# Attention of a streaming encoder step: token tiles taken in pairs of small and large, in groups of four heads

## The reference

```
q, k, v, z, qi, ki, wi = project(rmsnorm(h) @ w_in)       # 8 q heads, 2 kv heads, 8 indexer heads, head size 128
score = sum over indexer heads of wi * relu(qi . ki)      # one score for each query and key
sel   = top_k(score of keys in the query's 64-frame chunk or before, 256 keys; sample: 136)
o     = softmax(q . k[sel] * 128**-0.5) @ v[sel]          # each group of 4 q heads shares a kv head
h     = h + (o * silu(z)) @ w_out
```

## Time and profile before

| | before |
|---|---|
| time, median of 3 runs | 1431.69 us (1431.41 to 1433.59) |
| the profiled execution | 1432.42 us, its span 1430.6 us |
| PE busy | 1370.9 us (96%) |
| DVE busy | 907.0 us (63%) |
| ACT busy | 639.8 us (45%) |
| POOL busy | 671.7 us (47%) |
| attention, first q·k product to last product with v | 448.95 to 636.24 us |

### The profile page before, as it was taken

The page is one execution under the profiler, slowest core; times in us unless marked ns, Lnnn a source line. Parts: engine busy times, 40 slices in busy tenths (PEclk is TensorE's granted clock), DMA queues, the critical chain, the costliest instruction groups (busy, mean ns, idle before and its releaser), DMA issues.

```text
span 1430.6 us, 21114 instructions
## 1 busy us (share of the span) xinstructions
PE 1370.9 (96%) x7996; PEld 1193.2 (83%) x7996; DVE 907.0 (63%) x1638; ACT 639.8 (45%) x1125; POOL 671.7 (47%) x469
## 2 busy tenths in 40 slices
PE   5999999999998999989989999999999999999997
PEld 5999845999986555548879999999999999999786
DVE  4211287999994877533557676777676767677433
ACT  5333365678774655541114534343434343434111
POOL 2466700555554767740023656465656565654100
PEclk9999999999999999999999999999999999999999
DMA  7221100223222400002221101010101010106321
GB/s 226 87 58 45 44 1 1 60 76 93 69 64 75 147 15 20 0 30 84 87 84 48 45 21 60 22 60 22 60 22 60 22 60 21 60 7 208 108 88 67
DMA packets 101587, 86.79 MB, mean 61 GB/s; under 512 B 6480, under 2 KB 90320, under 8 KB 101488
## 3 DMA queue, kind: packets, MB, share of 16 engines
q1 hardware_dynamic: 99856, 80.63, 18.6%
q0 software_dynamic: 1632, 4.82, 0.9%
HBM read 65.46 MB, written 19.97 MB: 60 GB/s over the span
## 4 chain that ended last, share of the span: by engine, by line
PE 45%; DVE 7%; issue 1%; POOL 1%; DMA 1%; ACT 0%; SPq 0%; POOLq 0%; DVEq 0%; ACTq 0%
PE bank L186 27%; PE wide L1565 7%; PE bank L1460 7%; PE wide L1572 1%; DVE levels L1852 1%; DVE states L1888 1%; PE wide L1575 1%; DVE o_rec L1932 1%; DMA rw_raw<-in_rec_w_in 1%; PE wide L1548 1%; POOL o_sums L1764 1%; DVE log_decay L1820 0%; PE wide L1552 0%; DVE k_rec L1861 0%; DVE last_state L1888 0%
## 5 line engine op out<-in xcount | busy, mean ns | idle before, releaser
L186 PE MATMUL bank<-hn_hi,rw_hi 128*128 128x352 f32 x768 | 251.2, 327 | 6.7 <-DVE h_rows L1241 4.7
L186 PE MATMUL bank<-hn_hi,rw_lo 128*128 128x352 f32 x768 | 247.3, 322 | 0.0
L186 PE MATMUL bank<-hn_lo,rw_hi 128*128 128x352 f32 x768 | 247.0, 322 | 0.0
L186 PE MATMUL bank<-hn_hi,w_hi 128*128 128x352 f32 x648 | 210.3, 324 | 3.3 <-ACT relu L681 2.5
L186 PE MATMUL bank<-hn_lo,w_hi 128*128 128x352 f32 x648 | 207.8, 321 | 0.0
L186 PE MATMUL bank<-hn_hi,w_lo 128*128 128x352 f32 x648 | 207.7, 320 | 0.0
L950 POOL TENSOR_SCALAR probs<-probs,low 128x128 f32<-128x128 f32 (+8 forms) x72 | 127.6, 1775 | 63.3 <-DVE low L1085 63.1
L186 PEld LDWEIGHTS bank<-hn_hi,rw_hi 128*128 128x128 f32 x768 | 144.6, 188 | 8.8 <-DVE h_rows L1241 4.9
L186 PEld LDWEIGHTS bank<-hn_lo,rw_hi 128*128 128x128 f32 x768 | 145.1, 189 | 0.0
L186 PEld LDWEIGHTS bank<-hn_hi,rw_lo 128*128 128x128 f32 x768 | 144.6, 188 | 0.0
L730 POOL TENSOR_TENSOR swapped<-swapped,sin 128x352 f32<-128x352 f32 x57 | 55.4, 971 | 186.6 <-ACT swapped L677 125.8
(11 more groups left out here) (239 smaller groups left out, 2944.1 us busy)
## 6 DMA issues: line engine op xcount, KB each, us to landing
rw_raw<-in_rec_w_in SPq DMA_DIRECT2D x32, 512.0 KB, 4.0
w_raw<-in_att_w_in SPq DMA_DIRECT2D x27, 512.0 KB, 3.9
q_rotated<-relu SPq DMA_DIRECT2D x24, 176.0 KB, 1.9
xin<-in_x_prompt SPq DMA_DIRECT2D x8, 512.0 KB, 3.7
wo_raw<-in_att_w_out SPq DMA_DIRECT2D x4, 1024.0 KB, 8.5
x_again<-in_x_prompt SPq DMA_DIRECT2D x8, 512.0 KB, 4.2
residual<-h_rows SPq DMA_DIRECT2D x8, 512.0 KB, 2.9
wf_raw<-in_rec_w_out SPq DMA_DIRECT2D x4, 1024.0 KB, 10.2
```

The source lines that it names most:

```text
L186: last = pe.matmul(out, l, r, start=n == 0, stop=n == len(passes) - 1)
```

## The change

The list of items is built from groups of four heads: for each pair of tiles (0 and 7, 1 and 6, 2 and 5, 3 and 4) heads 0 to 3 of the small tile, heads 0 to 3 of the large one, heads 4 to 7 of the small one, heads 4 to 7 of the large one; the sample's two groups come last. Each group gets its queries by its own DMA of 256 KB. Groups 0 and 1 (heads 0 to 3 of tiles 0 and 7) are loaded when query head 6 is stored, groups 2 and 3 when all are, 4 to 7 after the first item, and from 8 on each when its buffer has been read; there are now eight query buffers of four heads, each with a semaphore. The buffers of groups 0 and 1 lie in new space behind the other tensors of the block. DVE marks tile 7 ahead of its first item, as soon as the rows of k are stored (L1073), and then, one step an item, tiles 6, 5, 2, 4, 3 and the sample. The work of an item is unchanged, and so are LAG, RING, the number of banks and the positions (48, 56; 52, 60) at which the output projection's weights are cast and split.

```diff
--- before.py
+++ after.py
@@ -132,7 +132,7 @@
         S["w_raw"] = space("w_raw", [P, W_SLOTS, KT, P])
         S["w_lo"] = Space(nc, w_at)("w_lo", [P, W_SLOTS, KT, P], F32R)
         S["w_hi"] = space("w_hi", [P, W_SLOTS, KT, P], F32R)
-        S["q_first"] = Space(nc, space.at)("q_first", [P, 2, HEADS, P])
+        S["q_first"] = [None, None] + [Space(nc, space.at + j * GROUP * P * 4)(f"q_first{2 + j}", [P, GROUP, P]) for j in range(2)]
         S["cos"] = space("cos", [P, T])
         S["sin"] = space("sin", [P, T])
 
@@ -267,6 +267,7 @@
     S["wi"] = space("wi", [P, NT, IH])
     S["kiTs"] = space("kiT_sample", [P, KEYS_S])
     S["signs"] = space("signs", [P, D], BF16)
+    S["q_first"][0:2] = [space(f"q_first{j}", [P, GROUP, P]) for j in range(2)]
     S["swapped"], S["relu"] = swapped, relu
     stages = [input_norm(nc, S), attention_project(nc, S), attention(nc, S)]
     with nc.Block() as block:
@@ -499,6 +500,7 @@
         after.setdefault(min(last_of_tile[c - SLOTS] + 2, last_of_tile[c - 1]), []).append(c)
 
 
+    EARLY = HEADS - 2
     BITS, PACE = 31, 5000
     rope_last = max(i for i, u in enumerate(units) if u[0] == "rope")
     counted_after, time = {}, 0
@@ -577,8 +579,16 @@
                     if i in rows_before:
                         store_rows(rows_before[i])
                 done = last_of_tile[c - SLOTS] + 1
+                if tiles[c - SLOTS] == EARLY * P:
+                    first = 3 * (EARLY + 1)
+                    sp.wait_ge(q_stored[0], 16 * ((first + 1) // 2))
+                    sp.wait_ge(q_stored[1], 16 * (first // 2))
+                    for group in range(2):
+                        load_queries(sp, S, group)
             for stored_q in q_stored:
                 sp.wait_ge(stored_q, 16 * n_q[N] // 2)
+            for group in range(2, 4):
+                load_queries(sp, S, group)
 
         def rows_stored(engine):
             engine.wait_ge(stored[0], 32 * ((NT + 1) // 2))
@@ -879,12 +889,27 @@
     return dict(sync=sync, tensor=tensor, scalar=scalar, gpsimd=gpsimd, vector=vector)
 
 
+def query_groups():
+
+    pairs = [(t, half) for small in range(NT // 2) for half in range(2) for t in (small, SAMPLE - 1 - small)]
+    return pairs + [(SAMPLE, 0), (SAMPLE, 1)]
+
+
+def load_queries(sp, S, group):
+
+    t, half = query_groups()[group]
+    sp.dma_start(S["queries"](group)[:, :, 0:rows(t)],
+                 S["q_dram"][GROUP * half:GROUP * (half + 1), :, span(t)].rearrange("h p t -> p h t")).then_inc(
+                     S["q_in"][group if group < 4 else 4 + group % 4], 16)
+
+
 def attention(nc, S):
 
     sem, ps, wide, pT, q_dram = S["sem"], S["ps"], S["wide"], S["pT"], S["q_dram"]
     gT, kT, v, ident = S["gT"], S["kT"], S["v"], S["ident"]
     kTs, cv, score, opened = S["kTs"], S["cv"], S["score"], S["open"]
-    items = [(t, h) for t in range(NT) for h in range(HEADS)]
+    groups = query_groups()
+    items = [(t, GROUP * half + h) for t, half in groups for h in range(GROUP)]
     N, LAG, RING = len(items), 4, 5
     masks, off = {0: opened[:, 0:P], 1: opened[:, P:3 * P]}, 0
     for t in range(2, NT):
@@ -907,37 +932,32 @@
     mixed, gated, order, inv_done = sem("mixed"), sem("gated"), sem("mark_order"), sem("inv_done")
     counts, limits, sel, bits, marks, ranks = (S[n] for n in ("counts", "limits", "sel", "bits", "marks", "ranks"))
     logits = wide[:].rearrange("p (s b) c -> p s (b c)", s=2)
-    q_in, wo_in = [sem("q_in0"), sem("q_in1")], sem("wo_in")
+    q_in, wo_in = [sem(f"q_in{j}") for j in range(8)], sem("wo_in")
+    S["q_in"] = q_in
     w_out = S["io"]["att_w_out"][0].rearrange("(k p) c -> p k c", p=P)
     space = Space(nc, S["lo_at"])
     probs = space("probs", [P, RING, SEQ])
     low = space("low", [P, 3, N])
-    q_next = space("q_tile", [P, 2, HEADS, P])
-    q_in_first = [sem("q_in_first0"), sem("q_in_first1")]
-
-    def queries(t):
-        return (S["q_first"] if t < 2 else q_next)[:, t % 2]
-
-    def wait_queries(engine, t):
-        if t < 2:
-            engine.wait_ge(q_in_first[t], 16)
-        else:
-            engine.wait_ge(q_in[t % 2], 16 * (t // 2))
+    q_next = space("q_tile", [P, 4, GROUP, P])
+    marked = [SAMPLE - 2] + [t for pair in range(2, NT // 2) for t in (SAMPLE - 1 - pair, pair)] + [SAMPLE]
+
+    def queries(group):
+        return S["q_first"][group] if group < 4 else q_next[:, group % 4]
+
+    S["queries"] = queries
     if True:
         def sync(sp):
-            for t in range(NT):
-                if t == 2:
+            for group in range(4, len(groups)):
+                if group == 4:
                     sp.wait_ge(logits_ready, 1)
-                elif t >= 4:
-                    sp.wait_ge(logits_ready, HEADS * (t - 1))
-                sp.dma_start(queries(t)[:, :, 0:rows(t)],
-                             q_dram[:, :, span(t)].rearrange("h p t -> p h t")).then_inc(
-                                 q_in_first[t] if t < 2 else q_in[t % 2], 16)
-                if t == 3:
-
-                    sp.wait_ge(logits_ready, 2 * HEADS)
+                if group == 8:
+
+                    sp.wait_ge(logits_ready, 4 * GROUP)
                     for ks, cols in weight_pieces():
                         sp.dma_start(S["wo_raw"][:, ks, cols], w_out[:, ks, cols]).then_inc(wo_in, 16)
+                if group >= 8:
+                    sp.wait_ge(logits_ready, GROUP * (group - 3))
+                load_queries(sp, S, group)
             S["rows_stored"](sp)
             sp.wait_ge(S["v_stored"], 32)
             sp.wait_ge(wo_in, 64)
@@ -962,12 +982,16 @@
                     pe.wait_ge(keys_done, 1)
                 if i >= 2:
                     pe.wait_ge(logits_read, i - 1)
-                if h == 0:
-                    wait_queries(pe, t)
+                group = i // GROUP
+                if i % GROUP == 0:
+                    if group < 4:
+                        pe.wait_ge(q_in[group], 16)
+                    else:
+                        pe.wait_ge(q_in[4 + group % 4], 16 * (group // 4))
                 src = kTs if t == SAMPLE else kT
                 for a in range(0, n, 512):
                     e = min(n, a + 512)
-                    last = pe.matmul(logits[0:rows(t), i % 2, a:e], queries(t)[:, h, 0:rows(t)],
+                    last = pe.matmul(logits[0:rows(t), i % 2, a:e], queries(group)[:, i % GROUP, 0:rows(t)],
                                      src[:, h // GROUP, a:e], start=True, stop=True)
                 last.then_inc(logits_ready, 1)
 
@@ -1069,15 +1093,15 @@
                                   gT[:, h:h + 4, span(t)], ALU.mult).then_inc(gated, 1)
 
             dve.wait_ge(S["open_done"], 3)
+            S["rows_stored"](dve)
+            for step in marking(SAMPLE - 1):
+                step()
             dve.wait_ge(*S["units_read"])
-            S["rows_stored"](dve)
+            steps = [step for t in marked for step in marking(t)]
             for i in range(N + 12):
                 if i < N:
-                    t, h = items[i]
-                    if h == 0 and 2 <= t + 1 < NT:
-                        steps = marking(t + 1)
                     shift(i)
-                    if 2 <= t + 1 < NT:
+                    if steps:
                         steps.pop(0)()
                 if 2 <= i <= N + 1:
                     t, h = items[i - 2]
```

## The result

The changed kernel takes 1444.51 us (median of 4 runs, 1443.01 to 1445.66), the kernel before 1432.21 (4 runs, 1431.41 to 1433.59). The ratio is 1.0077, 95% interval 1.0061 to 1.0092: slower by 12.3 us, where 6.7 were forecast. 1444.5 lies in the range (1431 to 1446), but above the forecast's own 1435 to 1441. The profiled execution took 1445.66 us around a span of 1443.9; the one before 1432.42 around 1430.6.

The account below looks back on a forecast made before the run. TensorE, busy 96% of the span, was taken as the bound. Attention: 444.67 + 169.3 work + 29.0 lost = 643.0, 6.7 us later, so 1432.42 + 6.7 - 0.7 = 1438.4 us; forecast 1435 to 1441, range 1431 to 1446.

Parts of the forecast that it names:

- opening: Steps 0 to 7 of attention, bound by VectorE: 4.4 us lost, with step 8 starting at 457.2.
- first switch: Steps 8 to 11, tile 7 to 0: transposes wait for GpSimd's large divisions; 13.6 us long, 8.4 lost.
- 7 to 1, 6 to 1, 6 to 2, 5 to 2: Later changes from large to small tiles: 11.6, 10.2, 10.3, 9.1 us long; 3.7, 2.0, 1.3 and none lost.
- all switches: All changes from a large to a small group in attention: together 15.4 us lost.
- casts: ScalarE's two casts of the output projection's weights, at steps 48 and 56: 1.8 us lost, bounds 0 and 3.8.
- tail from the last q·k: End of attention, behind the last q·k, with three sample divisions in line: 2.6 us lost.
- other steps: The other 40 prompt steps of attention at 0.12 us each: 4.8 us lost.
- the marks' waits: Waits for marks, named with the clock as what could come on top to reach the range's 1446.
- Free; without the cover, 8: VectorE's marking of tile 7 ahead of attention, from 435.9 to 444: no cost, or 8 us without the cover.
- I take it at nothing: TensorE's clock may fall in the opening, hidden beside VectorE's steps: cost nothing, bounds 0 and 2 us.
- slower still, by the clock: Rival: clock falls in the first switch; half clock costs 3.4 us, again behind tile 1; 1442 to 1445; chance 0.25.
- Faster: the pairs even out: Rival: GpSimd works ahead in attention, 16.5 us lost, 1425.9; decided at head 6's division by step 10; chance 0.12.

Follow-up runs that it names:

- a3: The changed kernel with GpSimd dividing only the first 128 columns of each head, the others left undivided: ratio 1.0003 to the kernel before.
- the control: The kernel before with GpSimd dividing only the first 128 columns of each head: ratio 0.9987 to the unedited kernel before.
- a2: The changed kernel with LAG 5 and RING 6, one step more between a head's q·k and its transposes: ratio 1.0031 to the kernel before.
- b1: The changed kernel without tile 7's marking ahead of attention, its scores going in as they are: ratio 1.0056 to the kernel before.
- c1: The changed kernel with its first four q·k products repeated 5, 8, 4 and 4 times to keep TensorE busy: ratio 1.0082 to the kernel before.
- a1: The changed kernel without the pairs and tile 7's early marking: old tile order, early queries per group; 1428.76 us, ratio 0.9949 to the kernel before.
- b4: The changed kernel with its first four groups' query loads all behind the last store, as before: ratio 1.0112 to the kernel before.

## Why the prediction was right in kind and short by 5.6 us

By its own steps, from the start of the first q·k; "lost" is length less PE's work as the prediction had it. The table follows the two profiled executions, which lie 13.2 us apart; the medians lie 12.3 apart.

| step | forecast | measured |
| --- | --- | --- |
| first q·k | 444.67, no DMA wait | 445.00, none |
| opening, lost | 4.4, step 8 at 457.2 | 8.75 (16.85 less 8.1), step 8 at 461.85 |
| first switch, lost | 8.4 (13.6 long) | 8.9 (14.13 long) |
| 7 to 1, 6 to 1, 6 to 2, 5 to 2, long | 11.6, 10.2, 10.3, 9.1 | 12.2, 10.6, 10.6, 9.4 |
| all switches, lost | 15.4 | 17.3 |
| casts | 1.8 | 0.95 (0.49 and 0.46, at 584.36 and 589.12) |
| tail from the last q·k, lost | 2.6 | 3.3 (9.0 long) |
| other steps | 4.8 | 3.9 (the rest) |
| sum, and the end | 29.0, 643.0 | 34.2, 648.51 |
| behind attention | 0 | 1.0 |

The mechanism was right. The reciprocal of the first large head comes some 1.2 us into step 8, as forecast, and its division 1.24; four large divisions follow in line, and the next large group has to wait for them; a3 takes this away and gains 8.7 us more than the control; a2, which only gives it more cover, gains 6.6. PE's waits were not spread as the prediction had them, 1.5 to 2 us in each of steps 9 to 11: 3.65 stand in step 8, none in step 9, 0.99 and 1.80 in steps 10 and 11. From tile 5 on there are none before the sample, as it said. The switches were 0.3 to 0.6 longer each than the sum. In the first the line of divisions was: from 465.93 (463.09 + 2.84) to 475.05 three took 9.1, not 8.5. From tile 7 to 1 it kept its 8.5 and started later, at 490.93, 2.6 us behind the last large q·k instead of 2.2. The range's 1446 has the marks' waits on top, a term that no run shows: all that the switches were over came to 1.9 (17.3 lost for 15.4).

**The term that was mis-sized is the opening, 8.75 for 4.4.** Three steps of its working failed, and b1 and c1 size them: b1's opening, without the marks and at the full clock, is 13.25 us long, c1's, at the full clock alone, 15.09, after's 16.85.

The first is "Free; without the cover, 8" on tile 7's marks: VectorE was idle there, but GpSimd was not, and its rotations and VectorE's marks took longer beside each other: L743 2.92 us beside the scan where b1 has 0.94, L1073 1.85 for 1.22. The marks ended at 447.7 and not at 444: four of them took 2.5 us more than the same marks in the kernel before, and the rest is that they started 0.3 late and were 9 us of work, not 8. The first shift stood 2.73 us behind the first q·k, for 0.94 in b1: 1.8 us of the opening. The earlier trace rows have both kinds of meeting. Beside GpSimd's division, a tensor_scalar, the mark kept its 1.22 and the division its 2.52; beside the 2.27 of VectorE's tensor_tensor a division took 4.49 for 2.52. The prediction hadn't asked what GpSimd does from 436 to 447: beside its tensor_tensor the same mark took 1.85. What makes both longer is not shown; the runs show the durations with and without the neighbour.

The second is "I take it at nothing" on the clock: it fell at 449.05, behind 4 us in which PE had about 1 us of work, and the first large q·k, with nothing in front of it to hide behind, took 1.8 us more. The opening is 1.8 longer than c1's, near the upper bound of 2 given. The two hang together: b1, without the marks, keeps the clock as well.

The third is that VectorE sets the pace of the opening throughout. Even in b1 it waits 0.96 us for the first large q·k, which can start only when VectorE has read the head two before it; b1's opening is 0.75 us longer than the forecast's. 1.8 + 1.8 + 0.75 is the 4.35 that the term was short.

The rival "slower still, by the clock" named the time, 1442 to 1445, and half of the reason. The clock did fall in the first switch (466.12, for 3.41 us), but the next large group ran at full speed (1.88 of modelled time at 475.98, 1.72 to the next), and the switch was 14.1 us with that fall, 13.8 in c1, where it lasted 6.83: there GpSimd's line hides it. What the clock cost lay in the opening. From attention's end on it is at 0.50 for 10.24 us from 647.03 (6.83 from 636.57 before) and for 6.83 from 759.67 (3.41 from 749.21 before); all that is behind attention took 1.0 more (795.4 for 794.4), and how much of that is the clock's wasn't taken apart.

"Faster: the pairs even out" failed where it was said to be decided: head 6's division was not done when step 10 wanted it. And the gain of the change, the queries, was sized right at 4 us for the old order (a1: attention ends 3.8 earlier); in the new order it is worth 5 (b4, uncertain by 4), where the last two rotations take 4.80 us beside the marks for 1.85, and late queries wait for the stores behind them.

## What to carry to other kernels

Before putting large and small items in turn, follow the slowest in-order engine through one change from large to small: with a lag of four items, a group of four large ones leaves its whole line of work to be waited for beside four that give no cover. An idle engine is a free place only if what runs beside it isn't slowed, as the rotation was here, from 0.94 to 2.92 us: list the neighbour's instructions in that stretch by their operands, and look for rows in which the same two kinds met. And where a new gap opens on TensorE, allow for the clock: here the first large product behind it took 3.55 us for 1.79. Last, read a difference in the total back to the stage that was edited, since c1's gain of 1.8 us there was gone at the end.

## What was not expected of the hardware

The same mark, scalar_tensor_tensor on 1024 columns, took 1.22 us beside a GpSimd tensor_scalar and 1.85 beside its tensor_tensor; GpSimd's tensor_tensor of 352 columns went from 0.94 to 2.92 us beside VectorE's scan, which itself took 3.00 (2.29 in the kernel before, where no GpSimd instruction ran beside it). The loss is on both sides. Which of the rotations pays changes from trace to trace: in c1 L743 kept its 0.93, and the two of L729 took 4.80 for 1.85.

The granted clock fell to 0.50 at 449.05 in the changed kernel, though PE hadn't been idle throughout: three small products ran in the 4 us before it. It stayed there for 6.83 us, and in other places and runs for 3.41 to 13.65 (the longest in b4, in its opening and from 649.58). With 17 small products in the same 4 us, the 34 instructions of c1's row, it stayed at 1.00.
